# Modulation tiles, rotation transfers and S5 preparation moved to other blocks of a one-core transformer kernel

## The reference

```
mods = einsum('bd,lde->lbe', silu(c), ada_w) + ada_b     # 4 layers of 3 x 1024 columns
kv_shift, kv_scale = split(silu(c) @ kv_ada_w + kv_ada_b)
# block 1: HGRN mixer, FFN 0, sparse attention, FFN 1; each on
#   rms_norm(x) * gain * (1 + scale) + shift, added to x times its gate
# block 2: differential attention (q and k normed and rotated),
#   MLP, S5 state-space layer with a gated projection, MLP
q = apply_rope_2(rms_norm_2(q, q_gain), cos, sin) * 64 ** -0.5
b_bar = ((exp(lam * dt) - 1) / lam)[..., None] * b_mat   # complex, per group of 16 channels
```

## Time and profile before

| | us |
|---|---|
| median of three runs | 3211.3 |
| profiled execution | 3211.83 |
| its span | 3210.1 |
| TensorE busy | 2902.5 (90%) |
| TensorE weight loads busy | 2345.2 (73%) |
| VectorE busy | 1683.1 (52%) |
| ScalarE busy | 1089.7 (34%) |
| POOL busy | 72.3 (2%) |

### The profile page before, as it was taken

One profiled execution on the slowest core, in us unless ns is written; L12 is line 12 of the kernel. 1 busy time (PEld: TensorE's weight loads), 2 busy tenths in 40 slices (PEclk: granted clock), 3 DMA queues, 4 the chain that ended last, 5 costly groups with the idle time before them and its releaser, 6 DMA issues.

```text
span 3210.1 us, 38764 instructions
## 1 busy us (share of the span) xinstructions
PE 2902.5 (90%) x14910; PEld 2345.2 (73%) x14910; DVE 1683.1 (52%) x2379; ACT 1089.7 (34%) x1540; POOL 72.3 (2%) x74
## 2 busy tenths in 40 slices
...
GB/s 187 176 152 1 115 153 183 172 183 111 121 105 94 1 1 1 1 66 90 101 91 85 121 112 40 1 98 107 138 144 151 230 79 92 66 79 95 89 104 66
DMA packets 407623, 321.16 MB, mean 100 GB/s; under 512 B 14034, under 2 KB 395068, under 8 KB 407484
## 3 DMA queue, kind: packets, MB, share of 16 engines
...
q0 software_dynamic: 1536, 4.20, 0.5%
...
## 4 chain that ended last, share of the span: by engine, by line
PE 77%; DVE 11%; ACT 5%; issue 4%; DMA 2%; ACTq 1%; POOL 1%; DVEq 0%; POOLq 0%
PE ps L435 51%; PE ps L417 6%; PE ps L429 4%; PE ps L847 2%; PE ps L2535 1%; DVE ada_ring L1687 1%; PE ps L833 1%; PE ps L820 1%; PE ps L1596 1%; PE ps L1561 1%; DVE ada_first L511 1%; DVE h_area L1691 1%; DVE h_area L1689 1%; ACT whi L385 1%; DVE ada_ring L497 1%
## 5 line engine op out<-in xcount | busy, mean ns | idle before, releaser
L435 PE MATMUL ps<-hh,whi 128*128 128x512 f32 x1744 | 690.2, 396 | 4.4 <-DVE xT L2368 1.6
L435 PE MATMUL ps<-hh,wlo 128*128 128x512 f32 x1744 | 680.2, 390 | 0.0
L435 PE MATMUL ps<-hl,whi 128*128 128x512 f32 x1744 | 679.5, 390 | 0.0
L389 DVE TENSOR_TENSOR wlo<-raw,whi 128x2048 fp32r<-128x2048 f32 x198 | 453.8, 2292 | 364.8 <-ACT whi L385 364.8
L385 ACT ACTIVATE whi<-raw 128x2048 fp32r<-128x2048 f32 x198 | 377.3, 1906 | 406.2 <-PE ps L435 257.8
L435 PEld LDWEIGHTS ps<-hh,whi 128*128 128x128 f32 x1744 | 328.1, 188 | 78.2 <-issue 11.8
L435 PEld LDWEIGHTS ps<-hl,whi 128*128 128x128 f32 x1744 | 328.1, 188 | 70.6 <-issue 3.8
L435 PEld LDWEIGHTS ps<-hh,wlo 128*128 128x128 f32 x1744 | 327.8, 188 | 69.2
L435 PE MATMUL ps<-hid_h,whi 128*128 128x512 f32 x756 | 307.2, 406 | 0.0
L435 PE MATMUL ps<-hid_l,whi 128*128 128x512 f32 x756 | 298.7, 395 | 0.0
L435 PE MATMUL ps<-hid_h,wlo 128*128 128x512 f32 x756 | 298.6, 395 | 0.0
...
## 6 DMA issues: line engine op xcount, KB each, us to landing
raw<-in_ffn_w_in SPq DMA_DIRECT2D x44, 1024.0 KB, 6.0
...
raw<-in_ffn_w_up SPq DMA_DIRECT2D x32, 1024.0 KB, 5.3
raw<-in_ffn_w_down SPq DMA_DIRECT2D x32, 1024.0 KB, 5.8
...
raw<-in_hgrn_w_in SPq DMA_DIRECT2D x16, 1024.0 KB, 5.8
raw<-in_attn_w_qkv SPq DMA_DIRECT2D x12, 1024.0 KB, 5.1
...
```

The lines of the kernel that those rows point to most:

```text
L389: nc.vector.tensor_tensor(wlo[:, par, :], raw[:, par, :], whi[:, par, :].bitcast(F32), ALU.subtract).then_inc(w_lo, 1)
L435: m = nc.tensor.matmul(ps[:, bank, :], tile(w, kt, j), x[:, kt, :], start=(kt == 0 and n == 0), stop=(kt == k - 1 and n == 2))
```

## The change

1. Modulation. Before, ffn0_in0 carries two tiles a block of layer 2 (22 tiles), ffn0_in1 two a block of layer 3 (22 tiles), n_q one a block (the last four of layer 3, two of them formed already). Now ffn0_in0 and ffn0_in1 carry one a block (tiles 0 to 21 of layer 2), ffn0_out1 two a block (16 tiles of layer 3) and n_q two a block (the last eight). ffn0_out0 and n_kvc keep their one. All in all 56 tiles for 58.
2. With two tiles a block, the two loads were each of four K tiles by 256 columns; now each is one tile, eight K tiles by 128 columns. VectorE's operations have the same count of elements, in two pieces of 128.
3. `d_turn` goes to SP. SP issues the turns of block t right after the weight load of block t + 4. The turns use two semaphores of earlier stages instead of two of their own, and wait for rotations only from block 4 on.
4. S5 preparation. What `prep_dve` did in block 6 goes to block 5. `PER_BLOCK` has one unit in blocks 6 and 7, where it had one in block 7 alone, and one instead of two in block 28.
5. The last evacuation has semaphores of its own, and its waits count from zero.

```
--- before.py
+++ after.py
@@ -247,7 +247,7 @@
         ada_step = sem("ada_step")
         ada_mm = sem("ada_mm")
         ada0_sum_v = sem("ada0_sum_v")
-        out_rdy, stored, out_ps = cols_rdy, sem("stored"), cols_ps
+        out_rdy, stored, out_ps = sem("out_rdy"), sem("stored"), sem("out_ps")
 
 
         def cols_of(w, first, step=256):
@@ -278,8 +278,8 @@
         def add_ffn1(layer):
             for half in range(2):
 
-                ada_in = ada_part(2 + half, 0, 2) if layer == 0 else None
-                ada = (a["kv_ada_w"], 8, 104, 1) if layer == 0 and half == 0 else None
+                ada_in = ada_part(2, 11 * half, 1) if layer == 0 else None
+                ada = ((a["kv_ada_w"], 8, 104, 1), ada_part(3, 0, 2))[half] if layer == 0 else None
                 add(f"ffn{layer}_in{half}", 11, pair_of(a["ffn_w_in"][layer], half * 11 * P), 1, 1, P, ada=ada_in)
                 add(f"ffn{layer}_out{half}", 8, rows_of(a["ffn_w_out"][layer], half * 11 * P, 11), 0, 1, P, 11, ada=ada)
 
@@ -305,7 +305,7 @@
             add("n_vs", 1, cols_of(w_kv, 768), 0, 2)
             add("n_kw", 1, cols_of(w_kv, 1024), 2, 0)
             add("n_vw", 1, cols_of(w_kv, 1280), 0, 2)
-            add("n_q", 4, cols_of(a["nsa_w_q"][0], 0), 2, 0, ada=ada_part(3, 20, 1))
+            add("n_q", 4, cols_of(a["nsa_w_q"][0], 0), 2, 0, ada=ada_part(3, 16, 2))
         if upto >= 7:
             add("n_out", 4, cols_of(a["nsa_w_out"][0], 0), 0, 2)
         if upto >= 8:
@@ -462,16 +462,15 @@
             fixed = isinstance(b, int)
             for slot, count, tile in ada_slots(s, b, par):
                 w, first = s.ada[0].rearrange("(k p) n -> p k n", p=P), s.ada[1]
-                k0, width = (4 * slot, 2 * P) if s.ada[3] == 2 else (0, P)
-                at = (tile - slot if s.ada[3] == 2 else tile) * P + first * P
+                at = tile * P + first * P
                 if not fixed:
                     at, count = act.snap(at), act.snap(count - 1)
                 elif count >= 2:
                     count = count - 1
                 if not (fixed and count < 2 and s.ada0 == 0 and tile < 2):
                     act.wait_ge(ada_used, count)
-                act.dma_start(ada_ring[:, slot, :].rearrange("p (k n) -> p k n", n=width),
-                              w[:, k0:k0 + D // width, bass.ds(at, width)]).then_inc(ada_in[slot], 16)
+                act.dma_start(ada_ring[:, slot, :].rearrange("p (k n) -> p k n", k=KT),
+                              w[:, :, bass.ds(at, P)]).then_inc(ada_in[slot], 16)
 
         def ada_sums(dve, s, b, par):
 
@@ -485,18 +484,15 @@
             if not isinstance(done, int) or done > 0:
                 dve.wait_ge(ada_mm, done)
             a0 = ada_sum_slot(s, par)
-            if per == 2:
-                w = ada_ring[:, :, :].rearrange("p s (k n) -> p (s k) n", n=2 * P)
-            else:
-                w = ada_ring[:, slots[0][0], :].rearrange("p (k n) -> p k n", n=P)
-            acc = ada_acc[:, a0:a0 + per, :].rearrange("p s n -> p (s n)")
-            nc.vector.tensor_scalar(w[:, 0, :], w[:, 0, :], cact[:, 0:1], None, ALU.mult).then_inc(ada_step, 1)
+            part = slice(0, 2) if per == 2 else slice(slots[0][0], slots[0][0] + 1)
+            w = ada_ring[:, part, :].rearrange("p s (k n) -> p s k n", k=KT)
+            nc.vector.tensor_scalar(w[:, :, 0, :], w[:, :, 0, :], cact[:, 0:1], None, ALU.mult).then_inc(ada_step, 1)
             for kt in range(1, KT):
                 dve.wait_ge(ada_step, b * (KT - 1) + (s.step0 + kt))
                 last = kt == KT - 1
                 nc.vector.scalar_tensor_tensor(
-                    out=acc if last else w[:, 0, :], in0=w[:, kt, :],
-                    scalar=cact[:, kt:kt + 1], in1=w[:, 0, :], op0=ALU.mult, op1=ALU.add
+                    out=ada_acc[:, a0:a0 + per, :] if last else w[:, :, 0, :], in0=w[:, :, kt, :],
+                    scalar=cact[:, kt:kt + 1], in1=w[:, :, 0, :], op0=ALU.mult, op1=ALU.add
                 ).then_inc(ada_used if last else ada_step, per if last else 1)
 
         def ada_first_dve(dve):
@@ -1033,7 +1029,7 @@
         D0 = {"d_q": 0, "d_k": 4, "d_v": 8}
         d_rot = nsa_area[:, 17664:21760].rearrange("p (k t) -> p k t", k=8)
         d_rs = nsa_area[:, 13568:17664].rearrange("p (k t) -> p k t", k=8)
-        turned_in = ((sem("turned_even"), 0), (sem("turned_odd"), 0))
+        turned_in = ((g_in, CMP_LOADS), (nsa_in, 80))
 
         def d_square(u):
             return (sq, xn)[u % 4 // 2][:, u % 2, :]
@@ -1041,14 +1037,14 @@
         def d_pair(db):
             return (dq, dk)[db // 4][:, 2 * (db % 4):2 * (db % 4) + 2, :]
 
-        def d_turn(pool, db):
-
-            pool.wait_ge(ev_a, seg["d_q"].ea0 + 2 * db + 2)
-            if db >= 2:
-                pool.wait_ge(dn_rot, RP0 + 2 * db - 2)
+        def d_turn(sp, db):
+
+            sp.wait_ge(ev_a, seg["d_q"].ea0 + 2 * db + 2)
+            if db >= 4:
+                sp.wait_ge(dn_rot, RP0 + 2 * db - 6)
             slots = slice(2 * db % 8, 2 * db % 8 + 2)
             for row in range(0, P, 32):
-                pool.dma_start(d_rot[row:row + 32, slots, :], d_pair(db)[row ^ 32:(row ^ 32) + 32, :, :]
+                sp.dma_start(d_rot[row:row + 32, slots, :], d_pair(db)[row ^ 32:(row ^ 32) + 32, :, :]
                              ).then_inc(turned_in[db % 2][0], 16)
 
         def d_hook_pe(pe, db):
@@ -1262,7 +1258,7 @@
         K5 = 7
         M5 = 6
         G0 = {"mlp0_in0": 0, "mlp0_out0": 8, "mlp0_in1": 16, "mlp0_out1": 24}
-        PER_BLOCK = [0] * 7 + [1] + [1, 2, 1, 2, 1, 2, 1, 2] + [1] * 8 + [2, 1, 2, 1, 2, 1, 1, 1]
+        PER_BLOCK = [0] * 6 + [1, 1] + [1, 2, 1, 2, 1, 2, 1, 2] + [1] * 8 + [2, 1, 2, 1, 1, 1, 1, 1]
         UNITS5, _n = [], 0
         for _k in PER_BLOCK:
             UNITS5.append([(u // NB5, u % NB5) for u in range(_n, _n + _k)])
@@ -1472,11 +1468,10 @@
                 d0 = ROWS["ssm_d_2"]
                 link(tt(gains_a[:, 5, :], cols_b[:, r0:r0 + 8], cols_b[:, d0:d0 + 8], ALU.mult))
             elif gb == 5:
+                tmp = tmp5.rearrange("p (h g) -> p h g", h=GH)
                 dve.wait_ge(s5_pp, 4)
                 tt(by_g(b_bar[:, 0, :, :]), taken(4), wide(wr), ALU.mult)
                 link(tt(by_g(b_bar[:, 1, :, :]), taken(4), wide(wi), ALU.mult))
-            elif gb == 6:
-                tmp = tmp5.rearrange("p (h g) -> p h g", h=GH)
                 dve.wait_ge(s5_pp, 5)
                 link(tt(tmp, taken(6), wide(wi), ALU.mult))
                 link(tt(by_g(b_bar[:, 0, :, :]), by_g(b_bar[:, 0, :, :]), tmp, ALU.subtract))
@@ -2011,10 +2006,15 @@
                         if b == 4:
                             s5_transfers(sp)
                         load(b, (s.g0 + b) % 2, True)
+                elif s.name in D0:
+                    for b in range(s.n):
+                        load(b, (s.g0 + b) % 2, True)
+                        if D0[s.name] + b >= 4:
+                            d_turn(sp, D0[s.name] + b - 4)
                 else:
                     each_block(sp, s, load)
 
-            sp.wait_ge(out_rdy, 2 * TT + 1)
+            sp.wait_ge(out_rdy, 2 * TT)
             sp.dma_start(out[0].rearrange("(t p) d -> p t d", p=P), xin[:, :, :]).then_inc(stored, 16)
             sp.wait_ge(stored, 16)
 
@@ -2035,8 +2035,6 @@
                 nc.gpsimd.memset(vblk.rearrange("p g n -> p (g n)"), 0.0).then_inc(vblk0, 1)
                 nc.gpsimd.memset(kcT[:, :, 31:32], 0.0).then_inc(vblk0, 1)
             if upto >= 9:
-                for db in range(8):
-                    d_turn(pool, db)
                 diff_pool(pool)
             if upto >= 11:
                 s5_pool(pool)
@@ -2495,7 +2493,7 @@
 
 
             for n in range(2 * TT):
-                dve.wait_ge(out_ps, n + 3)
+                dve.wait_ge(out_ps, n + 1)
                 nc.vector.tensor_copy(xin[:, n // 2, n % 2 * T:(n % 2 + 1) * T], ps[:, n % 4, :]
                                       ).then_inc(out_rdy, 1)
 
@@ -2646,7 +2644,7 @@
                 pe.wait_ge(ev_a, ea_end)
             for n in range(2 * TT):
                 if n >= 4:
-                    pe.wait_ge(out_rdy, n - 2)
+                    pe.wait_ge(out_rdy, n - 3)
                 for i in range(4):
                     kt = 4 * (n % 2) + i
                     m = nc.tensor.transpose(ps[:, n % 4, i * P:(i + 1) * P], xT[:, kt, n // 2 * P:(n // 2 + 1) * P],
```

56 lines of the change are left out of this document (27 added, 29 removed).

## The result

Four runs took 3253.11 to 3260.61 us, median 3256.6, where the kernel before took 3210.1 (four runs): +46.5 us, ratio 1.0152 (1.0133 to 1.0173). The forecast was 3240.5 with a range of 3223 to 3256. The sign and the waits that were named were right. One cost was sized at a third of what it is (the turns), and one was put at nothing (the form of the loads ahead of ffn0); the time lies just above the range. The profiled execution took 3260.06 (span 3258.2, 48.1 above that of before).

The account below looks back on a forecast made before the run. The prediction took TensorE, 77% of the chain of waits, to bound the kernel. Its terms, -5.3 + 21.7 + 1.0 + 5.5 + 6.3 = +29.2 us on 3211.3, gave 3240.5 us, range 3223 to 3256.

Parts of the forecast that it names:

- Part 1: ffn0_in: one modulation tile per block instead of two saves TensorE 0.24 us in each of 22 blocks, -5.3 us.
- Part 2: ffn0_out1: two tiles per block make a four-engine loop of 11.05 us set the pace, +21.7 us.
- Part 3: n_q: one more modulation tile per block in four blocks, pace stays TensorE's, +1.0 us.
- Part 4: d_q to d_v: turning DMAs on SP behind the weight load form a 14.5 us loop, +5.5 us.
- 5.2 + 2.05 = 7.25: Turns on SP: weight load's landing plus the turns' time on the engines, from load issue to turn landed, in us.
- The upper end of +12: Turns on SP: the cost from above, if load issue to turn landed takes 8 us.
- Part 5: S5 preparation a block earlier: TensorE waits 8.2 us for unit 0 instead of 2.90, plus lower clock, +6.3 us.
- Rival C: Contention: ffn0_out1 loop stretches to 12.5 us, turns land 8 us after their load; 3259 us, chance 0.10.
- up to +29: ffn0_out1: the upper bound, with a loop of 12 us from loads colliding with weight loads.

Follow-up runs that it names:

- e9: Changed kernel with old load form, turns ahead of weight load, ffn0_out1 loads ahead of the square, S5 units from block 8 on; 1.0041 against kernel before.
- e11: Kernel before with only the four S5 preparation operations of block 6 moved to block 5, units unmoved; ratio 1.0004.
- e12: e9 with the four S5 preparation operations put back in block 6; ratio 1.0021 against the kernel before.
- e5: Changed kernel with the old form of the modulation loads (four K tiles by 256 columns); 3247.4 us, 1.0123 against the kernel before.
- e1: Kernel before with only the form of the modulation loads changed to eight K tiles by 128 columns; 3223.45 us, ratio 1.0065.
- e7: Changed kernel with the next block's modulation loads in ffn0_out1 issued ahead of ScalarE's square; ratio 1.0134 against the kernel before.

## Why the prediction missed

By its steps, each against the traces of after and before:

- Part 1, -5.3 us: right. From the start of ffn0_in0 to that of ffn0_in1 are 189.0 us for 191.9, 2.9 less, and twice that is -5.8.
- Part 2, +21.7: right. ffn0 is 18.1 longer, so the loop cost 18.1 + 5.8 = 24. The period is 11.43 for 11.05: the form's share is 0.63 (I took 0.55), and the rest is the base, 10.8 for 10.5.
- Part 3, +1.0: not seen. n_q took 0.05 us more than before, n_kvc to n_vw 0.7 less.
- Part 4, +5.5: the loop right, the size wrong by a factor of three. The term that failed is "5.2 + 2.05 = 7.25" us from the load's issue to the turn's landing. From 1844.11 to the rotation at 1854.13 are 10.0 us, in the later blocks 8.1 to 9.0. I added the load's landing and the turns' share of the engines. But SP needs 2.5 us to issue the four turns, and the last lands another 5.0 to 6.1 us later (7.1 in the first block), beside the load. Over seven periods and the start that is some 11 us more for the loop. The clock wasn't in this part's sum at all: behind a wait of 3 us it is low for a while (row below), and the matmuls of this stretch took 8.0 us more, on top of 11.3 us of waits. The upper end of +12 came from 8 us and was too low as well.

```profile
1936.70:1951.50 14.80, 14.80 (x98) 14.56 (x99) 6.24 (x5) 1.69 (x2) 0.00 (x0) 0.79 0.40 107
```

- Part 5, +6.3: the number right, 6.3 in the trace, the account incomplete. The wait was put down to unit 0 alone; e9, e11 and e12 show a second one of 4.5 us inside it, for the low half of block 8's weights, which I had named only as hidden.
- Left out, the second step that failed: the form of the loads was priced in ffn0_out1 alone, and put at nothing from h_q to h_out without a reason, though these carry two tiles a block. It cost 10.7 us there in this trace, 10.1 when undone in e5, but 6.0 in e1 and 4.7 in e7. h_out was read as hidden because a block takes 13.36 us and the loop 11.2; its last block has no successor to hide behind, and its sums came 2.04 us late.
- Rival C came nearest in time, 3259, by half of its way: turns 8 us behind their load were near the measured 8.1 to 10.0, a loop of 12.5 us in ffn0_out1 was not (11.43).

The misses are 12.0 us in the turns and 10.7 in the first stage; ffn0 (+1.7) and n_q with its neighbours (-1.7) cancel by luck. Stages that the change doesn't touch took back 3.7 (-0.9 in the sparse attention, -2.8 behind mlp0). 29.2 + 12.0 + 10.7 - 3.7 = 48.2, for 48.1 in the spans. That the time lies within 1 us of the range's end is owed to the room left for ffn0_out1 (up to +29), where it wasn't needed. The ends as the prediction adds them up reach 3258; the range it gave stops at 3256.
